# A third gating projection moved into the first attention phase, its fillers moved behind it, and two sets of probability homes exchanged, in a two-layer attention, scan and expert kernel

## The reference, cut to what matters

```python
q, k, v, xs, bm, cm, z, dt_raw = project(h, w_in_l, conv_w_l, conv_b_l)
attn = attn_latent(q, k, v, kc, vc, sink_l)              # scores, exp, / denominator, times values
y = y_f + flip(y_b) + d_l * xs                           # the scan, both directions
g = y * silu(z)                                          # gated_rmsnorm: z is needed only here
g = g * rsqrt(mean(g * g) + EPS) * ssd_norm_w            # over each of two groups of 256
out = concatenate([attn, g]) @ w_out_l
# and, from the conditioning vector alone, for every layer:
sh1, sc1, g1, sh2, sc2, g2 = split(silu(c) @ w_ada_l + b_ada_l, 6)
```

## Time and profile before

| | us |
|---|---|
| median of 3 runs | 815.85 (813.15 to 817.71) |
| the profiled execution | 815.22, its span 813.5 |
| TensorE busy | 740.2, 91% of the span |
| VectorE, ScalarE, GpSimd busy | 328.2, 212.2, 142.7 |
| TensorE, from z of tile 2 to the end of attention, layer 0 | 122.60 to 170.82 |
| TensorE, from z of tile 2 to the first products of the scan, layer 1 | 510.78 to 561.20 |

### The profile page before, as it was taken

How to read it: one execution, slowest core, us unless ns; L and a number is a source line. 1 busy time by engine, 2 the same in 40 slices (tenths; PEclk the granted TensorE clock), 3 DMA queues, 4 the chain that set the end, 5 groups by cost and what they waited for, 6 DMA issues and landing times. The chain is left out here.

```text
span 813.5 us, 9343 instructions
## 1 busy us (share of the span) xinstructions
PE 740.2 (91%) x3420; PEld 372.5 (46%) x3420; DVE 328.2 (40%) x865; ACT 212.2 (26%) x484; POOL 142.7 (18%) x238
## 2 busy tenths in 40 slices
PE   3699998999998599999999999888999499999994
PEld 0347553446545344443344755345644344444331
DVE  1302625634734553211273163465643735331236
ACT  1301145923123101011133014593402311101121
POOL 2435032220000120000202402322001120000112
PEclk9799999999998699999999999999999989999998
DMA  8994335899700899999998223245420298999961
GB/s 334 395 354 172 110 110 213 318 348 405 295 1 27 324 370 365 421 423 423 410 326 314 104 104 110 104 151 210 183 104 0 93 413 356 414 423 422 423 253 78
DMA packets 54051, 211.54 MB, mean 260 GB/s; under 512 B 7883, under 2 KB 8755, under 8 KB 41715
## 3 DMA queue, kind: packets, MB, share of 16 engines
q1 hardware_dynamic: 40456, 179.33, 56.2%
q10 hardware_dynamic: 7851, 17.70, 5.6%
q0 software_dynamic: 5696, 13.89, 4.8%
HBM read 202.02 MB, written 13.93 MB: 265 GB/s over the span
## 5 line engine op out<-in xcount | busy, mean ns | idle before, releaser
L2150 PE MATMUL bank<-ring,work 128*64 128x512 f32 (+1 forms) x512 | 160.8, 605 | 2.7 <-DVE work L1537 1.7
L2150 PEld LDWEIGHTS bank<-ring,work 128*64 128x64 f32 (+1 forms) x512 | 60.3, 160 | 97.1 <-issue 94.6
L2166 PE MATMUL bank<-ring,xs_tok 128*64 128x512 f32 (+1 forms) x256 | 79.9, 597 | 3.4 <-DVE xs_tok L1548 3.4
L1548 DVE COPY xs_tok<-bank 128x256 f32<-128x256 f32 x22 | 9.3, 425 | 147.5 <-PE bank L2157 147.4
L1802 PE MATMUL bank<-hT,ring 128*128 128x384 f32 x192 | 62.2, 486 | 0.0
L1703 PE MATMUL bank<-ring,cpad 128*32 128x512 f32 x384 | 50.5, 653 | 8.3 <-DMA ring<-in_w_ada_dram 7.6
L1802 PEld LDWEIGHTS bank<-hT,ring 128*128 128x128 f32 x192 | 36.5, 190 | 25.0
L1770 PE MATMUL bank<-ring,hT 128*128 128x512 f32 x96 | 44.9, 625 | 2.3 <-ACT hT L799 2.3
L2166 PEld LDWEIGHTS bank<-ring,xs_tok 128*64 128x64 f32 (+1 forms) x256 | 27.9, 157 | 40.9 <-issue 35.4
L978 ACT ACTIVATE xs_tok<-bank 128x256 f32<-128x256 f32 x22 | 8.5, 386 | 140.2 <-PE bank L2150 140.2
L2051 PE MATMUL bank<-ring,xn 128*128 128x512 f32 x96 | 43.5, 596 | 0.0
(11 more groups left out here) (381 smaller groups left out, 1047.6 us busy)
## 6 DMA issues: line engine op xcount, KB each, us to landing
ring<-in_w_ada_dram SPq DMA_DIRECT2D x48, 1024.0 KB, 8.2
ring<-in_w_gate_dram SPq DMA_DIRECT2D x32, 1024.0 KB, 12.5
ring<-in_w_up_dram SPq DMA_DIRECT2D x32, 1024.0 KB, 15.6
ring<-in_w_down_dram SPq DMA_DIRECT2D x32, 1024.0 KB, 14.1
ring<-in_w_in_dram SPq DMA_DIRECT2D x16, 1024.0 KB, 15.5
ring<-in_w_out_dram SPq DMA_DIRECT2D x8, 1024.0 KB, 10.3
y_exp<-qkv ACTq DMA_DIRECT2D x16, 512.0 KB, 8.3
xpad<-gate_rows ACTq DMA_DIRECT2D x6, 512.0 KB, 5.2
```

The lines of the kernel that those rows point to most:

```text
L1548: dve.tensor_copy(hidT[:, b, :], bank[2][:, 0:F]).then_inc(s_htc, 1)
L2150: last = mm(bank[b][i * n:(i + 1) * n, :].rearrange("p (i f) -> p i f", i=2), rows_T[:, kt * P + i * n:kt * P + (i + 1) * n], gate_up_of(s ...
L2166: last = mm(bank[5 + hf][i * n:(i + 1) * n, :], hidT[:, b, f * P + i * n:f * P + (i + 1) * n], w[:, f, hf * 512:(hf + 1) * 512], start=f = ...
```

## The change

Z of tile 2 is no longer made in one piece before attention. Its eight matmuls stand in the first phase: three behind the scores of tile 0, one after each scores call of tile 1, and the last behind two transposes. The scores of tile 0 follow the sums of the decays at once. For this z of tile 2 gets bank 7; the sums of the decays move to bank 7 as well and must have been copied out before the first of its matmuls. As `hT` must hold the activations until then, the probabilities of tile 1 go to `xpad` and those of tile 2 to `hT`; `gm` and one state follow to `xpad`, `xw` goes to `hT`.

ACT copies this z out of the bank between the scalings of tile 0 and the exp of tile 1, without silu. Silu is done in place after the last exp of the decays, and a small exp behind it loads that table again. DVE's use of z waits for its own count of `s_zc`.

The units of the modulation that stood before and in the first phases move behind: none before the scores and none in the phase of tile 0, one at the end of the phase of tile 1 (layer 0), the rest in the phase of tile 2 and in the scan. F1 falls from 450 to 250, F2 from 550 to 350.

```diff
         probs = lambda t, h: (mixed[:, 1 + h // 4, h % 4 * P:(h % 4 + 1) * P] if t == 0 else
-                              (hT[:, h, :], xpad[:, h * NT * P:(h + 1) * NT * P])[t - 1])
+                              (xpad[:, h * NT * P:(h + 1) * NT * P], hT[:, h, :])[t - 1])
...
-        gm = ssd[:, 0:12 * P].rearrange("p (d t g c) -> p d t g c", d=2, t=NT, g=2)
+        gm = xpad[:, 0:12 * P].rearrange("p (d t g c) -> p d t g c", d=2, t=NT, g=2)
+        xw = [ssd[:, i * 512:(i + 1) * 512] for i in range(4)]
...
+        Z_BANK = (4, 5, 7)
+        cs_sum = bank[7][:, 0:96]
+        cs_psum = bank[7][:, 128:128 + 2 * P].rearrange("p (d c) -> p d c", d=2)
...
-        F0, F1, F2, F3 = 100, 450, 550, 1000
+        F0, F1, F2, F3 = 100, 250, 350, 1000
...
                 act.activation(wend[:, :, :, :], wend[:, :, :, :], ACT.Exp).then_inc(s_ecs, 1)
-                z_silu(2)
...
+                    if t == 0:
+                        act.wait_ge(s_z, NT * (l + 1))
+                        act.activation(mixed[:, 2, 512:1024], bank[Z_BANK[2]][:, :], ACT.Copy).then_inc(s_zc, 1)
...
+                act.wait_ge(s_zc, 4 * l + 3)
+                act.activation(mixed[:, 2, 512:1024], mixed[:, 2, 512:1024], ACT.Silu).then_inc(s_zc, 1)
+                act.activation(nm[:, 0, 0:1], one[:, :], ACT.Exp)
                 gates_stored(l)
...
+                pe.wait_ge(s_kvc, KV * l + KV_AT[1])
+                gating(0, 0, KT)
+                tokens()
+                pe.wait_ge(s_kvc, KV * l + KV_AT[2])
+                gating(1, 0, KT)
+                pe.wait_ge(s_xbcc, XM * l + 2)
+                decay_sums()
...
                 pe.wait_ge(s_qTc, 4 * (l + 1))
-                pe.wait_ge(s_zc, NT * (l + 1))
-                pe.wait_ge(s_cs, 2 * (l + 1))
-                fill(l, 100)
+                pe.wait_ge(s_xtc, 4 * l + NT)
+                pe.wait_ge(s_xbcc, XM * l + 1)
                 for j in range(4):
                     scores(0, j)
+                pe.wait_ge(s_cs, 2 * (l + 1))
+                gating(2, 0, 3)
...
-                        fill(l, F0 + (F1 - F0) * t // 3 + (F1 - F0) * (2 * j + 1) // 36)
+                        if t == 0:
+                            gating(2, 3 + j, 4 + j)
+                        elif t == 2:
+                            fill(l, F0 + (F1 - F0) * (2 * j + 1) // 9)
                         if j >= 2:
                             turned(t, 2 * j - 4)
                             turned(t, 2 * j - 3)
-                        fill(l, F0 + (F1 - F0) * t // 3 + (F1 - F0) * (2 * j + 2) // 36)
+                        if t == 0 and j == 3:
+                            gating(2, KT - 1, KT)
+                        elif t == 2:
+                            fill(l, F0 + (F1 - F0) * (2 * j + 2) // 9)
                     for i in range(4, H):
                         turned(t, i)
-                    fill(l, F0 + (F1 - F0) * (t + 1) // 3)
+                    if t == 1:
+                        pe.wait_ge(s_zc, 4 * l + 3)
+                    if t:
+                        fill(l, (F0, F1)[t - 1])
```

More of the change, by code:

```diff
@@ L165, in hybrid_step @@
         xdt = lambda d, t, g: halves[2 * (2 * t + d) + g]
-        xw = [xpad[:, i * 512:(i + 1) * 512] for i in range(4)]
-        b_tok = xpad[:, 4 * 512:4 * 512 + NT * P].rearrange("p (t c) -> p t c", t=NT)
+        b_tok = xpad[:, 12 * P:15 * P].rearrange("p (t c) -> p t c", t=NT)
         cs_rest = xpad[:, 0:2 * P].rearrange("p (d c) -> p d c", d=2)
@@ L173, in hybrid_step @@
         ssd = hT[:, :, :].rearrange("p k c -> p (k c)")
[L174 to L176 removed]
+        gm = xpad[:, 0:12 * P].rearrange("p (d t g c) -> p d t g c", d=2, t=NT, g=2)
+        xw = [ssd[:, i * 512:(i + 1) * 512] for i in range(4)]
+        init_st, next_st, final_st = (v.rearrange("p (d c) -> p d c", d=2)
+                                      for v in (xpad[:, 19 * P:23 * P], ssd[:, 16 * P:20 * P], ssd[:, 20 * P:24 * P]))
         qT = sb("qT", NT, 4, P)
@@ L235, in hybrid_step @@
         st_out = work[:, 2, :]
-        decay_at = (work[:, 3, :], qT[:, 0, :, :].rearrange("p a c -> p (a c)"), xpad[:, 2432:2944])
+        decay_at = (work[:, 3, :], qT[:, 0, :, :].rearrange("p a c -> p (a c)"), xpad[:, 15 * P:19 * P])
         fall_at = lambda k: max(2 * k, 1)
@@ L868, in z_silu @@
                     act.wait_ge(s_z, NT * l + t + 1)
-                    act.activation(mixed[:, t, 512:1024], bank[4 + t][:, :], ACT.Silu).then_inc(s_zc, 1)
+                    act.activation(mixed[:, t, 512:1024], bank[Z_BANK[t]][:, :], ACT.Silu).then_inc(s_zc, 1)
                 for i in range(NT):
@@ L1286, in finish @@
                     z = mixed[:, t, 512:1024]
+                    dve.wait_ge(s_zc, 4 * l + (1, 2, 4)[t])
                     step(dve.tensor_tensor(z, v, z, ALU.mult))
@@ L1852, in _, with gating @@
                 query_keys()
-                for t in range(NT):
-                    if t < 2:
-                        pe.wait_ge(s_kvc, KV * l + KV_AT[t + 1])
-                    else:
-                        pe.wait_ge(s_xbcc, XM * l + 1)
-                    for kt in range(KT):
-                        last = mm(bank[4 + t][:, :], tok(kt, t), slot(u + 3)[:, kt, :],
-                                  start=kt == 0, stop=kt == KT - 1)
-                    last.then_inc(s_z, 1)
-                    if t == 0:
-                        tokens()
-                    if t == 1:
-                        decay_sums()
+                z_weights = slot(u + 3)
+                def gating(t, first, end):
+                    for kt in range(first, end):
+                        last = mm(bank[Z_BANK[t]][:, :], tok(kt, t), z_weights[:, kt, :], start=kt == 0, stop=kt == KT - 1)
+                    if end == KT:
+                        last.then_inc(s_z, 1)
+                pe.wait_ge(s_kvc, KV * l + KV_AT[1])
[5 more added lines that the diff above has]
+                decay_sums()
                 u = OUT_AT[l]
```

11 lines of the change are left out of this document (4 added, 7 removed).

## The result

| | before | after |
|---|---|---|
| median of five runs of each, us | 817.27 (813.15 to 817.71) | 823.18 (822.49 to 824.63) |
| ratio, with its interval | | 1.007 (1.0036 to 1.0103) |
| profiled execution, us (span) | 815.22 (813.5) | 822.99 (821.2) |
| TensorE busy, us | 740.2 | 745.0 |

The account below looks back on a forecast made before the run. The kernel's time was taken as TensorE's work plus its idle time. Profiled 815.22 plus 0.2 idle and 3.0 clock gave 818.4; with the median 0.6 above the profiled run, 819.0 us was forecast, range 813.5 to 823.

Parts of the forecast that it names:

- within 0.5%: Whole kernel: measured time between 811.8 and 819.9 us, not told from no change; chance 0.59.
- slower by more: Whole kernel: slower by more than 0.5%, above 819.9 us; chance 0.33.
- First term: Before the third scores call of tile 0, TensorE waits 2.85 us for DVE's first mask, in each layer.
- Second term: Phase of tile 0: z done at 138.2, transposes wait about 0.28, scores of tile 2 begin at 139.4, 5.6 us earlier.
- Third term: Phase of tile 1: TensorE waits 1.6 before the transposes, then 0.89 for ACT and 0.29 for DVE; 2.8 us in sum.
- Fourth term: Phase of tile 2: waits for DVE's copies, two in layer 0, three in layer 1, 0.28 each; 0.65 before the values.
- Fifth term: Scan: layer 1's wait of 1.49 us before the first products goes, covered by a unit; layer 0 nothing.
- ledger of idle time: Attention and scan: layer 0 7.1 against 4.5, +2.6 us; layer 1 7.4 against 9.75, -2.4; together +0.2.
- Transfers: Scan of layer 0: fifth unit lands 0 to 1.1 us late, taken as nothing; late-transfer rival 817 to 823, chance 0.08.
- The gates: Output projection: silu and table loads move ACT's gate rows some 2.3 us, to 208; covered by projection, cost nothing.
- The clock: Behind the hole in attention: TensorE's clock may fall, costing 0 to 3.4 us a layer; taken 1.5 each, +3.0.
- rival of two full falls: Clock falls in each hole and stays for 6.8 us, 3.4 lost per layer: 822.9 us, chance 0.13.

Follow-up runs that it names:

- e2: The changed kernel with the decays' sums in bank 3 and z's first three steps between the second and third scores calls of tile 0: 813.30 us, ratio 0.9943.
- e3: The changed kernel with z's new order kept and units of the modulation put back, mainly in the phase of tile 1: 814.77 us, ratio 0.9956 to before.
- e6: The changed kernel without silu of tile 2's z and the small exp behind it, that computation left out: 823.59 us, ratio 1.008 to before.
- e5: The kernel before, with only the units of the modulation moved behind and z in its old place: 821.71 us, ratio 1.0052.
- e7: e4 with z's last five steps in one block behind the scores of tile 0: 813.32 us, ratio 0.9947 to before.
- e4: The changed kernel with the edits of e2 and e3 together: 805.81 us, ratio 0.9862 to before.

## Why the prediction was right, and where it was off

The forecast was 819.0, 3.2 above the median then known. Measured were 823.2, 5.9 above the median of the five runs of before, and a ratio of 1.007; on the forecast's own base of 815.85 this ratio gives 821.6. So the kernel is slower as forecast, by nearly twice as much. The likeliest outcome was "within 0.5%" (0.59); "slower by more" had 0.33. Of the range the median passed the upper end, 823, by 0.2.

- **First term, the hole: right.** 2.79 measured for 2.85, released by DVE's mask in both layers. e2 shows that it can be filled.
- **Second term, the phase of tile 0: 2 us short.** z was done 17.6 us after the start, not 15.6. Of this 1.7 is the clock (3.4 us at the lower level). The rest is the interleaving: a scores call and a step of z take 1.90 from start to start (131.65 to 133.55, say), not 0.78 + 0.88 = 1.66. I had priced both by their rows in a run.
- **Third term, the phase of tile 1: right in layer 0.** 1.64 + 0.88 + 0.30 = 2.82 for 2.8. In layer 1 it is 1.64 + 0.21: the second fall of the clock slows the transposes ahead, and the wait of 0.89 is used up by it. Layer 1's rows foretold layer 0's. My fear that a later arrival would hide the wait did not come true, since ACT's copy waits for the same last step of z. No run sets this copy elsewhere, so what its place costs stays open.
- **Fourth term: right** in 0.65 before the values.
- **Fifth term, the scan: right in layer 1** (no wait at 568.59), **wrong in layer 0**, where a unit came 1.83 late.
- **The ledger of idle time: right.** -0.16 for +0.2; to the points of the earlier trace rows 7.3 and 6.8 us idle for 7.1 and 7.4. What one layer wins the other loses. It is luck in part: layer 1 stands at 6.8 and not at 7.4 because the wait of 0.89 above was used up by low clock, which the ledger doesn't count.
- **Transfers: the step that failed in kind.** I worked out that the fifth unit would land between 0 and 1.1 us late and took nothing. It landed 1.8 late, at 201.86 instead of 199.9. The rate wasn't at fault: SP issues the first of the five at 172.42, where I had 170.9, as the unit that frees its slot ends only then; from there five units take 29.4 us, 5.9 each for my 5.8. TensorE came for the fifth at 200.03 where I had 198.8. So the step that failed is the start of the chain and the choice of nothing out of 0 to 1.1. e3, which uses units earlier, has no such wait; e2, which doesn't, has 1.91. The gates: ACT's row comes 8.1 us later, 5.9 with the whole scan and 2.2 for the 2.3 that I had for silu and its loads; the wait of DVE comes from the landing (e6), and it costs nothing, for the cover of projection held.
- **The clock: the term that was mis-sized.** 1.5 a layer was forecast; slower work took 5.6 in sum (steps included). The low stretches sum to 13.6 us, 6.8 lost at half speed, a part of it in waits, where it costs nothing. That is the price of the rival of two full falls, but in other places: in this trace one short fall at the hole of layer 0, a full one at that of layer 1 and a second fall behind it. Over the four profiles with the hole the clock is low for 6.8 us in six of its eight cases and for 3.4 in two, so the full fall is the usual one and my 1.5 was too little; and I had priced the hole alone. The second fall comes behind the wait of 1.64, and those of e5 in the phase of tile 0 behind 1.58 and 1.57, where fillers were taken away. The Trainium skill (TensorE: Matmul & The Clock Gate, "HAM oscillation — how this bites in real kernels") gives as its rule that TensorE should have no long idle gaps. In e7 it isn't enough to keep to this: its clock fell with no wait over 0.85 in the 5 us before.

So the sum is: idle time -0.2, clock and slower steps +5.6, weights +1.8, together 7.3 of the 7.7 in the span. The runs then split the change by its halves, if not quite cleanly, as e3 also gathers in the phase of tile 1 the units that stood ahead of it. Moving z with the units kept in attention (e3) is faster than before by 0.4%; moving the units alone (e5) is slower by 0.5%; both (after) are slower by 0.7%. So the halves don't add up: the units' move costs 0.5% by itself and 1.1% on top of z's. z's move pays in full (e4, 1.4% faster) when its first steps fill the hole that it makes.

## What to carry to other kernels

When dense work is taken from a place, ask first what it covered: z of tile 2 covered DVE's splitting, and the units covered ACT's exp. A filler in a sparse stretch can pay three times, by the idle time that it fills, by the clock that it holds up, and by the buffer that it frees for the next transfer; moved to where TensorE is full, it loses the last two even when the idle time comes out even. Before such a move look for a few steps of real work whose bank is free at the moment of the hole.

## What the runs showed of the hardware that was not expected

- The clock fell to its lower level without a long wait: in e7 TensorE was busy 1.66 of the 3 us before the fall, with waits of 0.21 to 0.85. The same happened in layer 1.
- The same kernel's clock fell at the same hole for 3.4 us in one execution and for 6.8 in another, and the gap of 1.74 before the router brought a fall in the profile of after and none in that of its repeat. A single trace doesn't tell what a wait costs in clock.
- In e5 (clock 0.53 from 202.4 to 206.0) the unit behind the wait of 2.07 for weights took 3.62, as it ran at the lower clock, where in after, behind 1.83, it took 1.92. The same wait is paid twice in one execution and once in another.
- The row of a single step of z (128x512, fp32) shows 1.12 or 1.13 between scores calls at full clock, against 0.88 for each of a run, but rows overlap: from its start to the start of the scores behind it is 1.06, and a block of five takes 0.90 a step (e7).
- With the list of weights late, the loads of the gates took 9.45 us from issue to the end of DVE's wait, where before they had landed within 6.2.
